# Branch A's queries of tokens 256-511 projected late, between the first merges and weighings

## What is computed

```
n = rms_norm(h) * (1 + scale1) + shift1
aq, ak, av, iq, ik, iw, bq, bk, bv, cq, ck, cv, cr, ca, gl = split(n @ w_in)
# A: per head of 64: q = rms_norm(aq, gain_q), k = rms_norm(ak, gain_k); an indexer picks the top 128 keys of a token
logits = q . k / 8 on the picked keys;  ya = softmax(logits) @ av
merged = sum_b sigmoid(gl_b + b_gate_b) * (y_b @ w_o_b);   h = h + gate1 * (merged @ w_out)
n2 = rms_norm(h) * (1 + scale2) + shift2
# PEER: 8 heads, each: scores of n2 @ w_pq against 2 x 128 keys, top 16 of their sums -> 16 experts
h = h + gate2 * sum over 128 experts of  share * gelu(n2 . u[expert]) * v[expert]
```

## Time and profile before

| | us |
|---|---|
| median of 3 executions | 2057.0 (2055.41 to 2059.61) |
| the profiled execution | 2055.41 |
| its span in the profile | 2053.6 |
| busy PE / DVE / POOL / ACT | 1667.6 / 1454.6 / 633.5 / 576.0 |
| mean DMA rate over the span | 321 GB/s (658.72 MB) |

### The profile page before, as it was taken

The page is one execution under the profiler, slowest core; times in us unless marked ns, Lnnn a source line. Parts: engine busy times, 40 slices in busy tenths (PEclk is TensorE's granted clock), DMA queues, the critical chain, the costliest instruction groups (busy, mean ns, idle before and its releaser), DMA issues.

```text
span 2053.6 us, 17698 instructions
## 1 busy us (share of the span) xinstructions
PE 1667.6 (81%) x5546; PEld 926.8 (45%) x5546; DVE 1454.6 (71%) x3352; ACT 576.0 (28%) x1263; POOL 633.5 (31%) x542
## 2 busy tenths in 40 slices
PE   4999999999888898998988667767877676667676
PEld 3443445667777465565655333333443222222222
DVE  5346551668316888887787998877777878887876
ACT  2111122665214442542222223222222222212221
POOL 0000000120002343433334454544444544345441
PEclk8999999999999999999999878888898988788888
DMA  9442120011346999999999999999999999999995
GB/s 372 182 177 96 57 112 30 31 73 51 137 183 277 418 418 420 410 416 407 414 396 420 419 420 379 419 420 419 420 419 420 420 419 420 420 419 420 420 419 240
DMA packets 89806, 658.72 MB, mean 321 GB/s; under 512 B 9952, under 2 KB 11120, under 8 KB 16240
## 3 DMA queue, kind: packets, MB, share of 16 engines
q0 software_dynamic: 73728, 536.90, 63.4%
q1 hardware_dynamic: 14336, 119.18, 14.6%
q10 hardware_dynamic: 1648, 1.51, 0.2%
HBM read 653.95 MB, written 3.34 MB: 320 GB/s over the span
## 4 chain that ended last, share of the span: by engine, by line
DMA 37%; PE 35%; DVE 14%; issue 8%; ACT 4%; POOL 2%; SPq 0%; DVEq 0%; POOLq 0%; PEldq 0%; ACTq 0%
DMA sb<-uv_table,sb 35%; PE ps L1076 10%; PE ps L647 6%; PE ps L649 4%; DVE sb L1959 3%; DVE sb L1983 2%; PE ps L754 2%; POOL sb L2110 2%; PE ps L998 2%; PE ps L959 1%; PE ps L1003 1%; DMA sb<-w_mod 1%; PE ps L926 1%; PE ps L768 1%; PE ps L585 1%
## 5 line engine op out<-in xcount | busy, mean ns | idle before, releaser
L1076 PE MATMUL ps<-sb 128*128 128x512 f32 x1424 | 779.7, 693 | 289.8 <-ACT sb L1453 285.6
L2110 POOL DMA_INDIRECT sb<-uv_table,sb x512 | 606.5, 1185 | 879.8 <-PE ps L1076 663.7
L1959 DVE CUSTOM_DVE_ANT_0 sb<-sb 128x1024 f32<-128x1024 f32 x512 | 625.6, 1222 | 243.2 <-DMA sb<-uv_table,sb 235.7
L1076 PEld LDWEIGHTS ps<-sb 128*128 128x128 f32 x1424 | 294.7, 219 | 720.2 <-ACT sb L1453 413.2
L1453 ACT ACTIVATE sb<-sb 128x128 f32<-128x128 f32 x356 | 132.1, 397 | 601.2 <-DVE sb L1968 590.7
L1983 DVE SCALAR_TENSOR_TENSOR sb<-sb 128x512 f32<-128x512 f32 x304 | 214.8, 748 | 2.2
L1442 ACT ACTIVATE sb<-sb 128x2 f32<-128x2 f32 x256 | 51.7, 202 | 411.6 <-DVE sb L1959 408.3
L2076 POOL TENSOR_TENSOR sb<-sb 128x128 f32<-128x128 f32 x8 | 13.1, 1637 | 435.0 <-DVE sb L1704 435.0
L647 PE MATMUL ps<-sb 128*128 128x512 f32 x304 | 137.8, 606 | 0.0
L959 PE MATMUL ps<-sb 128*128 128x256 f32 (+1 forms) x576 | 114.8, 352 | 0.2 <-DMA sb<-w_pq 0.2
L959 PEld LDWEIGHTS ps<-sb 128*128 128x128 f32 x576 | 97.5, 191 | 28.5 <-issue 17.4
(11 more groups left out here) (267 smaller groups left out, 1773.8 us busy)
## 6 DMA issues: line engine op xcount, KB each, us to landing
sb<-w_mod SPq DMA_DIRECT2D x11, 2048.0 KB, 13.0
sb<-w_pq SPq DMA_DIRECT2D x18, 1152.0 KB
sb<-w_merge SPq DMA_DIRECT2D x24, 768.0 KB
sb<-w_proj SPq DMA_DIRECT2D x8, 2048.0 KB, 8.4
sb<-w_merge SPq DMA_DIRECT2D x6, 2304.0 KB, 9.0
sb<-w_out SPq DMA_DIRECT2D x8, 1024.0 KB, 9.3
sb<-uv_table,sb POOLq DMA_INDIRECT x512, 27.6
sb<-w_merge SPq DMA_DIRECT2D x3, 1536.0 KB, 8.0
```

Source lines behind the costliest of these rows:

```text
L1076: mm = pe.matmul(bank(2 * (t % 2) + f), dgw[m % NDG], row_v(n)[:, T * f:T * (f + 1)], start=(i == 0), stop=(i == PH * PK - 2))
L1959: dve.tensor_tensor_reduce(out=row_u(n), in0=row_u(n), in1=n2_tm(u // PH), scale=1.0, scalar=0.0, op0=ALU.mult, op1=ALU.add, accum_out=dot ...
L2110: pool.indirect_dma_start(out=ring[PLACE[n]], out_offset=None, in_=uv_table, in_offset=bass.IndirectOffsetOnAxis(ap=experts[u % 4][:, i:i ...
```

## The change

Branch A's queries of jobs 0 to 3 are projected for tokens 0-255 only; their copies, squares, square sums, spreads and scalings are half as wide. The queries of tokens 256-511 come later, from n_t's second half, in four pieces of two heads (`late_query`, 8 products of 128x256 each): pieces 0 and 1 on PE behind the first late merge and ahead of `squares_sum(1)`, piece 2 in slot 0, piece 3 in slot 2. ACT copies a pair of pieces with the gain as scale and squares them (`late_query_out`; for pair 0 between `half_gate(0)` and `square(1)`); PE sums the squares per head into 8 columns (`late_query_sums`), DVE makes the factors (`late_query_var`, `late_query_factors`), ACT the root. The queries are not scaled: the factor stands as `scale` in the exponential and in its bias, and the score is no longer scaled by 1/8 (the sum has no 1/64 either).

Only one merge stays ahead of the slots; the second moves to slot 3. The weights of the queries, w_proj[0], are loaded a second time: three pieces (1.57 MB) behind the three w_out loads and ahead of merge 8, the fourth (0.52 MB) once piece 2 has been used. qa is no longer saved and loaded back. The w_out pieces take ring slots 3 to 6 in place of 4 to 7, so gathers 3 to 6 wait for the output (`yo_done`) and gather 7 waits for pieces 0 and 1.

```diff
-        wo_first = ring[4:8]
+        wo_first = ring[3:7]
+        wq_late = [ring[7][:, 0:KT * P], ring[7][:, KT * P:2 * KT * P], area("ya", 2 * T, KT * P), area("ya", 2 * T, KT * P)]
...
+        def job_cols(j):
+            return H if jobs[j][1] == 0 else T
...
-        EARLY_MERGES = 2
+        EARLY_MERGES = 1
         MERGE_SLOT = {slot: EARLY_MERGES + i for i, slot in enumerate(
-            [4, 7, 8, 11, 12, 15, 16, 19, 20, 22, 23, 24, 26, 27, 28, 29, 30, 31, 32, 33, 34, 35])}
+            [3, 4, 7, 8, 11, 12, 15, 16, 19, 20, 22, 23, 24, 26, 27, 28, 29, 30, 31, 32, 33, 34, 35])}
...
+        LATE_QUERY_AT = {0: 2, 2: 3}
+        LATE_SQ_AT, LATE_VAR_AT, LATE_ROOT_AT, LATE_R_AT = 3, 4, 5, 6
...
                     if i == 8:
                         sp.wait_ge(s["co_done"], 1)
-                        for p in (0, 2, 3):
+                        for p in (0, 1, 3):
                             sp.dma_start(wo_first[p], w_out[:, 2 * KT * P * p:2 * KT * P * (p + 1)]).then_inc(wo_first_in[p], 16)
+                        sp.dma_start(ring[7], w_proj[0][:, 0:2 * KT * P]).then_inc(s["ql_in"], 16)
+                        sp.dma_start(wq_late[2], w_proj[0][:, 2 * KT * P:3 * KT * P]).then_inc(s["ql_in"], 16)
...
-            sp.wait_ge(s["kept_out"], 5 * 16)
-            sp.dma_start(area("w", KEPT, 3 * T), kept[:, 0:3 * T]).then_inc(s["kept_in"], 16)
-            sp.dma_start(area("w", late + T, 896), kept[:, 3 * T:3 * T + 896]).then_inc(s["kept_in"], 16)
+            sp.wait_ge(s["kept_out"], 3 * 16)
+            sp.dma_start(area("w", KEPT, 2 * T), kept[:, 0:2 * T]).then_inc(s["kept_in"], 16)
+            sp.dma_start(pen_h(2), kept[:, 2 * T:2 * T + 384]).then_inc(s["kept_in"], 16)
...
             merge_weights(3)
-            merge_weights(4)
+            sp.wait_ge(s["proj_done"], NJ + 3)
+            sp.dma_start(wq_late[3], w_proj[0][:, 3 * KT * P:4 * KT * P]).then_inc(s["ql_in"], 16)
...
-                        mm = pe.matmul(bank(b), w[:, i, k, :], n_t[:, k, :], start=(k == 0), stop=(k == KT - 1))
+                        n = job_cols(j)
+                        mm = pe.matmul(bank(b, n), w[:, i, k, :], n_t[:, k, 0:n], start=(k == 0), stop=(k == KT - 1))
...
+            def late_query(i):
+
+                pe.wait_ge(s["ql_in"], 48 if i == 3 else 32)
+                if i == 2:
+                    pe.wait_ge(s["yg_ready"], 4)
+                w = tiles(wq_late[i], KT)
+                for k in range(KT):
+                    mm = pe.matmul(bank(3 + 2 * (i // 2), H, H * (i % 2)), w[:, k, :], n_t[:, k, H:T],
+                                   start=(k == 0), stop=(k == KT - 1))
+                mm.then_inc(s["proj_done"], 1)
+
+            def late_query_sums(pair):
+
+                pe.wait_ge(s["sq_ready"], N_STAT + pair + 1)
+                for t in range(2):
+                    for i in range(2):
+                        mm = pe.matmul(bank(3 + 2 * pair, 2, 4 * t + 2 * i), sq_late[:, H * i + P * t:H * i + P * (t + 1)],
+                                       area("const", C_SEL, 2), start=True, stop=True)
+                mm.then_inc(s["sq_used"], 1)
...
             merge_products(0)
+            late_query(0)
+            late_query(1)
             squares_sum(1)
...
             score(2)
-            merge_products(1)
+            late_query_sums(0)
...
+            def late_query_out(pair):
+                act.wait_ge(s["proj_done"], NJ + 2 * pair + 2)
+                b = bank(3 + 2 * pair)
+                for qt in range(2, TT):
+                    act.activation(q_h(qt)[:, 2 * pair:2 * pair + 2, :], tiles(b, 2)[:, :, P * (qt - 2):P * (qt - 1)], ACT.Copy,
+                                   scale=vcol(V_GAIN))
+                if pair == 1:
+                    act.wait_ge(s["sq_used"], N_STAT + 1)
+                act.activation(sq_late, b, ACT.Square).then_inc(s["sq_ready"], 1)
...
             half_gate(0)
+            late_query_out(0)
             square(1)
...
-                act.activation(p, p, ACT.Exp, bias=anmax[:, i:i + 1], accum_out=asum[:, i:i + 1]).then_inc(s["prob_ready"], 1)
+                if j in (0, 4):
+                    act.wait_ge(s["stat_r"], 3 + j // 4)
+                act.activation(p, p, ACT.Exp, scale=ql_col(j), bias=anmax[:, i:i + 1], accum_out=asum[:, i:i + 1]).then_inc(s["prob_ready"], 1)
...
             variance(1)
+            late_query_var(0)
             dot(4)
             dot(5)
             normed(1)
+            late_query_factors(0)
             weights(2)
-            half_merge(1)
...
-                elif 4 <= PLACE[n] < R_EARLY:
+                elif 3 <= PLACE[n] < 7:
                     pool.wait_ge(s["yo_done"], 4)
+                elif PLACE[n] == 7:
+                    pool.wait_ge(s["proj_done"], NJ + 2)
```

More of the change, by code:

```diff
@@ L389, in encoder_layer @@
                    tm_done tm_out g2t_ready g2_done g2_ready picked p_step dot_done gelu_ready ex_ready
-                   share_ready w_ready dg_ready weighed gated2 added stored halved mh_used dve_weighed pen_ready kept_out kept_in""".split()
+                   share_ready w_ready dg_ready weighed gated2 added stored halved mh_used dve_weighed pen_ready kept_out kept_in ql_in""".split()
         row_in = [sem(f"row_in{i}") for i in range(len(ring))]
@@ L613, in square_sums, with spread @@
                 sel = area("const", C_SEL + 16 * t, 16)
-                pe.matmul(bank(b, T, 0, 0, 16), sel, sq[i % 2], start=(t == 0), stop=(i in (4, N_STAT - 1)))\
-                  .then_inc(s["sq_used"], 1)
-            def spread(done, i, t):
+                n = H if i < 4 else T
+                pe.matmul(bank(b, n, 0, 0, 16), sel, sq[i % 2][:, 0:n], start=(t == 0), stop=(i in (4, N_STAT - 1)),
+                          skip_group_check=True).then_inc(s["sq_used"], 1)
+            def spread(done, i, t, n=T):
                 sel = area("const", C_SELT + P * t, P, 0, 16)
-                pe.matmul(bank(4 + i % 2), sel, st_r, start=True, stop=True).then_inc(done, 1)
+                pe.matmul(bank(4 + i % 2, n), sel, st_r[:, 0:n], start=True, stop=True).then_inc(done, 1)
             def spread_b(t):
@@ L675, in _ @@
                         pe.wait_ge(s["xa_read"], t - 1)
-                    spread(s["xa_done"], t, t)
+                    spread(s["xa_done"], t, t, H if t < 4 else T)
                 for m in INDEX_AT.get(j, ()):
@@ L1139, in _ @@
                             score(q)
+                if slot in LATE_QUERY_AT:
+                    late_query(LATE_QUERY_AT[slot])
+                if slot == LATE_SQ_AT:
+                    late_query_sums(1)
                 if slot in MERGE_SLOT:
@@ L1195, in project_out @@
                     else:
-                        c = act.activation(o, bank(b), ACT.Copy, scale=scale)
+                        c = act.activation(o, bank(b, w), ACT.Copy, scale=scale)
                     if stat is not None:
@@ L1236, in _ @@
             act.dma_start(kept[:, 0:T], ka).then_inc(s["kept_out"], 16)
-            act.dma_start(tiles(kept[:, 2 * T:3 * T], 4), qa[:, :, 3 * P:4 * P]).then_inc(s["kept_out"], 16)
-            act.dma_start(tiles(kept[:, 3 * T:4 * T], 4), qa[:, :, 2 * P:3 * P]).then_inc(s["kept_out"], 16)
             NA = NF
@@ L1266, in _ @@
             act.dma_start(kept[:, T:2 * T], pen(3)).then_inc(s["kept_out"], 16)
-            act.dma_start(kept[:, 4 * T:4 * T + 384], pen(2)).then_inc(s["kept_out"], 16)
+            act.dma_start(kept[:, 2 * T:2 * T + 384], pen(2)).then_inc(s["kept_out"], 16)
             def gate(n):
@@ L1492, in _ @@
                     exponents(u + 1)
+                if slot == LATE_ROOT_AT:
+                    late_query_root(1)
                 if slot in LATE_SUM or part == 1:
@@ L1498, in _ @@
                     scores_out(QUERY_SLOT[slot - 2])
+                if slot == max(LATE_QUERY_AT):
+                    late_query_out(1)
                 if slot in MERGE_SLOT:
@@ L1852, in late_sum, with late_query_var, late_query_factors @@
                 dve.wait_ge(s["pt_done"], i - 1)
-                dve.tensor_tensor_reduce(out=prob_h(j), in0=bank(2, n), in1=pen_h(qt), scale=HD ** -0.5, scalar=-3.4e38,
+                dve.tensor_tensor_reduce(out=prob_h(j), in0=bank(2, n), in1=pen_h(qt), scale=1.0, scalar=-3.4e38,
                                          op0=ALU.add, op1=ALU.max, accum_out=amax_h(j)).then_inc(s["la_read"], 1)
                 dve.wait_ge(s["la_read"], i + 1)
-                dve.tensor_scalar(anmax[:, i:i + 1], amax_h(j), -1.0, None, ALU.mult).then_inc(s["nmax_ready"], 1)
+                dve.tensor_scalar(anmax[:, i:i + 1], amax_h(j), ql_col(j), -1.0, ALU.mult, ALU.mult).then_inc(s["nmax_ready"], 1)
+            def late_query_var(pair):
+                dve.wait_ge(s["sq_used"], N_STAT + pair + 1)
+                dve.tensor_scalar(ql_var[:, 8 * pair:8 * pair + 8], bank(3 + 2 * pair, 8), 1.0, HD * EPS, ALU.mult, ALU.add)\
+                   .then_inc(s["stat_var"], 1)
```

(9 more changed lines are left out.)

36 lines of the change are left out of this document (24 added, 12 removed).

## The result

The changed kernel takes 2071.3 us (median of 6 runs, 2065.41 to 2073.79) where the kernel before takes 2056.6 (6 runs beside it, 2055.41 to 2059.61). The ratio of the runs is 1.0064, with a 95% interval of 1.0046 to 1.0082. It is slower, as forecast, but by 14.7 us where the sum said 6.7; the median lies 0.3 us above 2071, where the forecast's range ended. (The forecast counted from a median before of 2057.0; the ratio laid on it gives 2070.2.) The profiled executions stand at 2069.54 and 2055.41 us, with spans of 2067.7 and 2053.6: +14.1 us.

A forecast was written before the change was run, and what follows sets the result against it. It took a PE chain to bound the kernel up to the first gather, then a DMA stream whose lost time is not made up. -15.2 + 3.8 + 18.1 = +6.7 us gave 2063 us, range 2048 to 2071.

The forecast's parts named there:

- Part 1: Early chain through PE: half-width jobs, square sums and spreads were to save 15.2 us, bounds 11 and 17.5.
- another 1.7 us goes there: PE at the stream's start, waiting for the dots: some 5 us idle, then records at the lower clock level, 1.7 us.
- Rival (d): The early saving is short: w_mod piece 4 us late, or halved jobs cost more than half; 2067 to 2070; chance 0.07.
- Part 2: Two loads put ahead of merge 8 in SP's queue lengthen PE's wait for it: +3.8 us, bounds 3.7 and 4.6.
- Part 3: Start of the gather stream: late queries delay square(1) and gather 16, opening two DMA gaps; stream 18.1 us later.
- slot 4 on has the old work: Late slots on PE: after merge 1 and the sums in slot 3, work is as before; no cost counted.
- Scale and bias operands of late_exp cost nothing: ACT's exponential of the late attention: the added scale and bias operands were put at no cost.
- (a): At the stream's start, the stream takes the delay in; only 1.25 us of bytes remain: -10.1 us, 2046; chance 0.15.
- (b): Only the gap after the first eight gathers opens: 7.9 + 1.25 instead of 18.1, -2.3 us, 2054 to 2055; chance 0.2.
- (c): wq_late[3], requested after late_query(2), takes 15 us and PE stands 5 us: sum +12, 2069; chance 0.08.
- The forecast's own case: Whole kernel: the summed +6.7 us, said as 2063, spanning about 2058 to 2068; chance 0.5.
- The rule on columns: Early projection by the clock gate page's spacings: halving columns saves only a quarter of the job, 7 us instead of 14.

The follow-up runs named there:

- experiment 4: Kernel before with only the half width of jobs 0 to 3, queries of tokens 256-511 never made: 2043.75 us, ratio 0.9928.
- experiment 10: Changed kernel with jobs 0 to 3 at full width again, so all the late work and no early saving: 2081.36 us, ratio 1.0118.
- experiment 6: experiment 5 plus piece 2 ahead of the first weighing, piece 3 in slot 3, merge 1 in slot 4, a later merge in slot 21: 2050.30 us.
- experiment 2: Changed kernel with the two w_proj loads issued behind merge 8 instead of ahead of it: 2061.72 us, ratio 1.0026.
- experiment 1: Changed kernel with late queries 0 and 1 and their copies moved behind score(2): 2064.95 us, ratio 1.0026.
- experiment 8: Changed kernel with the 16 products of query pieces 2 and 3 left out, all waits, loads, copies and sums kept: 2060.98 us.
- experiment 7: Changed kernel with merge 1 in slot 4 instead of 3, later merges one place later each, one in slot 21: 2072.07 us.
- experiment 3: Changed kernel with DVE making the factors (inverse root) ahead of the fourth sum over w_mod: 2065.29 us, ratio 1.0043.
- experiment 5: Changed kernel with the edits of experiment 1, experiment 2 and experiment 3 together: 2055.69 us, ratio 0.9999.
- experiment 11: experiment 6 with the second pair's square sums behind the merge of slot 4: 2049.07 us, ratio 0.9964.
- experiment 9: Kernel before with DVE making the factors ahead of the fourth w_mod sum, as a control: 2057.47 us, ratio 0.9997.

## Why the prediction was right in kind and short in size

**The two parts** (a chain to the first gather, a stream behind it whose losses stay) held. Experiments 4 and 10 bear them out: an early saving and a late loss each arrive at the end, to within 2 us. And the order of the late work matters: it alone took the stream's loss from 20.3 to 7.3 us (experiment 6).

**Part 1, the early projection: the term that was mis-sized.** Counted -15.2 us, measured -11.1 at the job at 117 us. The widths, the wait and its three causes were right to within 0.8 us; the other 3.4 are two jobs at the lower clock level behind the wait. The prediction costed such a slow stretch at a later place, "another 1.7 us goes there", and left it out here, where PE waits as well. Rival (d) asked for the same shortfall of 4 to 8 us but from other causes, the w_mod piece or the halved jobs; the piece took 7.67 us, as counted, and the jobs halved. At 469 us another product behind a wait of 2.78 us was slow by 1.6 us, and when SP reaches the loads of merge 8 (553.60) the saving was 10.2. This 1.6 isn't the change's: see the last section.

**Part 2, merge 8:** counted 3.8, measured 4.0, in the changed kernel and, as a difference, in experiments 2 and 10.

So the first gather came 6.2 us earlier, not 11.4: 5.2 of the 7.4 us by which the profiles' difference (14.1) misses the sum (6.7). The forecast had named this as a sign of being wrong, and by it the early part was wrong in size.

**Part 3, the start of the stream.** Counted +18.1, measured +20.3. Gather 16 was to come 66 us behind the first and came 66.7; square(1) 17 us behind and came 17.2; gather 8 needed 38.5 us, 38.2 by the forecast's 671.5. The gaps are 10.7 and 6.7 us, forecast 8 and 9. Most of this difference lies in how the forecast split its 17: its first gap ends when gather 8 is issued, without the 1.8 us from issue to transfer that it adds for gather 16. With them it is 9.8 and about 7. The mechanism is the stated one: experiment 1 takes most of the first gap away by order alone, experiment 8 takes the second away by PE's work alone.

**The step that failed in part 3** is "slot 4 on has the old work", from which no cost was drawn. The work is old, but there PE waits 3.21 us for `late_sum` at 721.93 (1.27 and 0.68 us at the two such places before, 709.39 and 720.74) and then runs two groups of records 3.1 us slower than at the higher level. That makes the third loss, some 2 to 3 us of the stream's 20.3. Why they were slow here stays open.

**A term put at nothing.** "Scale and bias operands of late_exp cost nothing": ACT's exponential of 128x384 took 0.62 us before and takes 0.71 with the scale operand, 0.09 us more in each of 16, 1.5 us of ACT. Nothing shows that it reaches the end.

**The rivals.** (a), that the stream takes it in, is out: the rate fell to 100 and to 21 GB/s. (b), only the first gap, is out by the second gap at 690 us; experiment 8, in which the second gap is absent, shows about what (b) would have been, +9.8 us of stream where (b) said 9.2. (c) is out: `late_query(3)` at 687.74 follows on the job ahead of it without a wait for wq_late[3], which landed 8.3 us behind its issue at 678.27; that left only 1.2 us. (d) has the right size and the wrong causes.

**What was luck.** The forecast's own case ended at 2068. The range went on to 2071 for (c) and (d), and neither of their causes occurred; that the measured time comes out so close to its end is not a merit of the sum.

**The rule on columns.** In the changed kernel PE is 14.9 us earlier at the spread, where half-width jobs at the spacings of the Trainium skill ("TensorE: Matmul & The Clock Gate", "Back-to-back issue gap") would have given about half of the 14 us of the jobs. The measurement decides: in this float32 kernel 16 records of 256 columns take half the time of 16 of 512.

## What to carry to other kernels

Work that is moved off a full stage lands in another, and there its place in each engine's order decides: the same products cost 20 us of stream in one order and 7 in another. Count how long the transfers in flight last against the time until the next one can be released; beyond that, each microsecond ahead of the release is lost: what this stream had lost by gather 28 it had lost at the end. And where a sum makes an engine early for another, price the wait and also the slower records that may follow it: here 1.3 to 2.1 us of wait and up to 4.6 of slower jobs.

## What was not expected of the hardware

A short wait of PE was followed in some places by records at the lower clock level, and their loss was in part longer than the wait. Ahead of the spread PE waits 1.3 to 2.1 us for DVE in the changed kernel and in experiments 1, 2, 4, 7 and 8. The next two jobs of 16 records took:

| kernel | first job, us | second job, us |
|---|---|---|
| changed | 8.77 | 8.77 |
| experiment 1 | 9.94 | 8.77 |
| experiment 2 | 8.98 | 7.08 |
| experiment 4 | 9.91 | 8.77 |
| experiment 7 | 8.77 | 7.08 |
| experiment 8 | 8.46 | 7.08 |

In each at least the first is slow. With the order of experiment 3 both took 7.08 in experiments 3, 5 and 6, but 7.08 and 8.77 in experiment 11, where PE has no other wait there than the 0.48 us for ACT that it has in all of them, the kernel before included. So the long wait makes the slow job likely, and isn't its only condition.

A second place shows how little the wait alone decides. One product of a merge (at 469.11 us in the changed kernel, 480.20 before) follows on a wait of 2.78 us for DVE in all thirteen kernels. It took 3.72 us in four of them (before, experiments 2, 3 and 10) and 5.17 to 5.41 in the other nine, experiment 9 among them, which is the kernel before but for one order on DVE. So 1.6 us between two profiles can come from here without any edit, and a single profile can't price it.

The Trainium skill says in "TensorE: Matmul & The Clock Gate", under "What's actually happening", that the throttled state is the default and activity releases it. The rows agree in that most slow records stand behind a pause, and show at 469 us that the same pause gives either level. How much of the spread between the runs of one kernel comes from it was not shown.
